# Summing gathered rows of v in runs of eight instead of four, beside the first half of the second block

## What is computed

```python
def peer_ffn(h, wq, sub_keys, u, v):
    def block(t):                                   # t: 128 tokens of width D = 1024
        ...                                         # 8 heads choose 16 experts each: idx, g
        a = jax.nn.gelu(jnp.einsum('tpkd,td->tpk', u[idx], t).astype(jnp.float32), approximate=False)
        return jnp.einsum('tpk,tpkd->td', (g * a).astype(t.dtype), v[idx])
```

## Time and profile before

| | us |
|---|---|
| median of 3 timed runs | 2850.53 |
| lowest and highest of them | 2850.36, 2853.51 |
| the profiled execution | 2857.94 |
| its span, first to last instruction | 2856.1 |
| TensorE busy with matmuls | 2311.2 (81%) |
| VectorE busy | 1887.5 (66%) |
| GpSimd busy | 1086.1 (38%) |
| all matmuls of L1939 (2048 records, tiles 0 to 3): idle time ahead of them for a landing | 271 |

### The profile page before, as it was taken

How to read it: one execution, slowest core, us unless ns; L and a number is a source line. 1 busy time by engine, 2 the same in 40 slices (tenths; PEclk the granted TensorE clock), 3 DMA queues, 4 the chain that set the end, 5 groups by cost and what they waited for, 6 DMA issues and landing times.

```text
span 2856.1 us, 43515 instructions
## 1 busy us (share of the span) xinstructions
PE 2311.2 (81%) x16384; PEld 1719.6 (60%) x16384; DVE 1887.5 (66%) x4182; ACT 899.6 (31%) x1615; POOL 1086.1 (38%) x1029
## 2 busy tenths in 40 slices
PE   7999988877565554665847988875999999999998
PEld 5787876445311010112736877622777999997998
DVE  3666885786565666537898877763444687667766
ACT  4555652111100000001013333322333455456544
POOL 0000002544466676667886676576555000000000
PEclk8999999988777787777968999867999999999999
DMA  7432126787799999999999999999999545662564
GB/s 303 152 124 85 38 83 246 288 335 282 298 374 374 356 376 355 336 356 342 401 359 400 404 408 409 410 376 337 388 391 408 194 155 191 189 210 89 184 189 152
DMA packets 225231, 810.32 MB, mean 284 GB/s; under 512 B 24704, under 2 KB 30720, under 8 KB 223232
## 3 DMA queue, kind: packets, MB, share of 16 engines
q0 software_dynamic: 147456, 536.94, 49.2%
q1 hardware_dynamic: 76992, 270.09, 26.5%
q10 hardware_dynamic: 576, 0.52, 0.1%
HBM read 805.35 MB, written 2.10 MB: 283 GB/s over the span
## 4 chain that ended last, share of the span: by engine, by line
PE 42%; DVE 17%; issue 11%; another core or an unknown queue 5%; DMA 5%; POOL 2%; ACT 1%; DVEq 0%; POOLq 0%; SPq 0%; ACTq 0%
PE ps L2004 10%; PE ps L2005 10%; PE ps L2006 9%; DVE pe_ring L2847 7%; PE ps L1939 6%; DMA pe_ring<-in_v,pe_vidx 2%; DMA pe_ring<-in_u,pe_idx 2%; PE ps L1894 1%; DVE la_w_lo L2900 1%; POOL pe_ring L1826 1%; PE ps L2087 1%; DVE pe_itop L2774 1%; POOL pe_ring L1832 1%; PE ps L2312 1%
## 5 line engine op out<-in xcount | busy, mean ns | idle before, releaser
L1826 POOL DMA_INDIRECT pe_ring<-in_u,pe_idx x415 | 462.6, 1115 | 297.4 <-issue 117.4
L1939 PE MATMUL ps<-pe_ring,pe_spot 128*32 128x512 f32 x1620 | 378.8, 728 | 172.3 <-DMA pe_ring<-in_v,pe_vidx 110.0
L1832 POOL DMA_INDIRECT pe_ring<-in_v,pe_vidx x405 | 417.1, 1030 | 224.0 <-issue 115.8
L2004 PE MATMUL ps<-la_h_hi,la_w_hi 128*128 128x256 f32 x1696 | 481.7, 284 | 9.6 <-issue 4.7
L2005 PE MATMUL ps<-la_h_lo,la_w_hi 128*128 128x256 f32 x1696 | 477.7, 282 | 2.9 <-issue 2.9
L2006 PE MATMUL ps<-la_h_hi,la_w_lo 128*128 128x256 f32 x1696 | 477.8, 282 | 2.6 <-issue 2.6
L2900 DVE TENSOR_TENSOR la_w_lo<-la_w_raw,la_w_hi 128x1024 fp32r<-128x1024 f32 (+1 forms) x348 | 415.5, 1195 | 87.6 <-ACT la_w_hi L2469 61.9
L2469 ACT ACTIVATE la_w_hi<-la_w_raw 128x1024 fp32r<-128x1024 f32 (+1 forms) x348 | 359.0, 1032 | 281.4 <-DMA la_w_raw<-in_down 89.0
L2004 PEld LDWEIGHTS ps<-la_h_hi,la_w_hi 128*128 128x128 f32 x1696 | 322.6, 190 | 38.0 <-issue 27.5
L2005 PEld LDWEIGHTS ps<-la_h_lo,la_w_hi 128*128 128x128 f32 x1696 | 320.2, 189 | 5.1 <-issue 4.8
L2006 PEld LDWEIGHTS ps<-la_h_hi,la_w_lo 128*128 128x128 f32 x1696 | 320.3, 189 | 3.9 <-issue 3.9
(11 more groups left out here) (409 smaller groups left out, 3911.5 us busy)
## 6 DMA issues: line engine op xcount, KB each, us to landing
la_w_raw<-in_gate SPq DMA_DIRECT2D x88, 512.0 KB
la_w_raw<-in_up SPq DMA_DIRECT2D x88, 512.0 KB
la_w_raw<-in_down SPq DMA_DIRECT2D x64, 448.0 KB
la_w_raw<-in_a_in SPq DMA_DIRECT2D x40, 512.0 KB
wring<-in_w_in SPq DMA_DIRECT2D x32, 512.0 KB
la_w_raw<-in_down SPq DMA_DIRECT2D x32, 512.0 KB
wring<-in_wq SPq DMA_DIRECT2D x22, 512.0 KB, 7.4
xT<-in_w_mod_rows SPq DMA_DIRECT2D x8, 1024.0 KB, 4.9
```

The source lines that it names most:

```text
L1826: pool.indirect_dma_start(row(n), None, io["u"], bass.IndirectOffsetOnAxis(idx[:, t, j:j + 1], 0)).then_inc(land[GATHERS[n][0]], 16)
L1832: pool.indirect_dma_start(row(n), None, io["v"], bass.IndirectOffsetOnAxis(vidx[:, t % 2, at:at + 1], 0)).then_inc(land[GATHERS[n][0]], 16)
L1939: return pe.matmul(ps[PER * grp:PER * grp + PER, half, :], spot[:, j // TOKENS % 2, grp, lo:lo + PER], row(n)[:, half * 512:(half + 1) * 5 ...
L2004: pe.matmul(slot(n), parts_hi[:, n % SPLIT, i, :], hi[:, k, :], start=first, stop=False)
```

## The change

`sums_beside` takes 16 runs of eight rows for each of the tiles 2 and 3 in place of 32 runs of four. A run is due when its eighth row is. The sums of tiles 0 and 1 stay as they are. `SQUARES_AT`, the row of tile 3 at which `add_squares(2)` is due, goes from 58 to 56, a multiple of eight.

```diff
--- before.py
+++ after.py
@@ -1446,7 +1446,7 @@
     CHOOSE_AT, CHOOSE_V = (25, 51, 77, 103), 9
     HEAD, IN_PSUM = 26, 8
     AHEAD, STEP, LAG = 14, 3, 5
-    TURN_AT, SUM_AT, SQUARES_AT = (96, 84), (16, 32), 58
+    TURN_AT, SUM_AT, SQUARES_AT = (96, 84), (16, 32), 56
 
     def gathers():
 
@@ -1971,9 +1971,9 @@
                 yield DOTTED[2] + 3 * STEP
                 turn_weights(2)
                 for t in (2, 3):
-                    for j in range(0, P, GROUPS):
-                        yield sum_at(t, j + GROUPS - 1)
-                        sum_rows(t, range(j, j + GROUPS))
+                    for j in range(0, P, 2 * GROUPS):
+                        yield sum_at(t, j + 2 * GROUPS - 1)
+                        sum_rows(t, range(j, j + 2 * GROUPS))
 
             def turns_beside():
                 yield DOTTED[3] + 3 * STEP
```

## The result

The changed kernel takes 2925.45 us (median of 6 runs, 2914.72 to 2928.76) against 2852.02 us of the kernel before (6 runs, 2842.53 to 2860.52). The ratio is 1.025 with a 95% interval of 1.0231 to 1.0269: 66 to 77 us slower, where 40 were forecast and 2925 was the upper end of the range. The profiled execution of the changed kernel took 2927.72 us (span 2925.9).

A forecast was written before the change was run, and what follows sets the result against it. Row transfers were taken to bound the kernel up to 1846 us, TensorE the last tile. Full stage +26, beside attention +19, last tile -5 made +40 on 2850.5: 2890 us, range 2843 to 2925.

The forecast's parts named there:

- 3 rows under way: In tile 2, when a run of eight's last row lands: 3 rows (3.8 us) may be under way, before 11 (14 us).

The follow-up runs named there:

- the later release: Against the changed kernel, a run of eight releases all its slots with its last matmul, not one by one; 1.03 times the kernel before.

## What to carry to other kernels

Where a ring of buffers feeds a stage that is full of transfers, count how many transfers may be under way at the moment a consumer gets its last one, and hold it against one turn: start to release, release to issue, issue to landing. Well above it fewer buffers cost nothing here (8 rows in place of 11), well below it each consumer run costs idle transfers (3.9 us each here), in every run of the full stage, also where no wait shows before the change. A consumer that is reached late takes from the same number, even if it finds all its rows landed. Joining two consumer steps takes from this number twice: the rows of the second step are no longer ahead, and those of the first are not given back.

## What the runs showed of the hardware

- A row lands with the last of the 16 DMA engines, and the others can be a row ahead. At 1749 us three rows were still to land, the last at 1752.7, and yet the DMA share was 0.35 from 1750 to 1751, 0.06 from 1751 to 1752, which is one engine of 16, and 0.01 from 1752 to 1753. So 3 rows under way kept the engines as a whole busy not for 3.8 us but for about 1.5. Why one engine came last is open.
- The Trainium skill ("DMA: Bandwidth & Descriptors", "Anatomy of one DMA") says that a semaphore is raised only once the write is confirmed, which takes most of 2 us. The trace does not bear out that length: the last packet of those rows ended at 1752.3, 0.4 us ahead of the last landing, and 0.4 to 0.5 us lay between the two at most other stops of the two traces of after and of the later release.
- The first row behind a stop took 3.8 to 5.8 us from issue to landing, where the data alone is 1.3 us at full rate. At 1754.87 and at about half of the other stops 1.6 us went by before its first packet moved; with the 0.4 us at the end that is about 2 us in which nothing moves, and the packets themselves took the rest.
- TensorE, which had stood for 11.5 us, began the run of 1749.03 at a granted clock of 0.50, the lower of its two levels (1.2 of 2.4 GHz), and was at 1.00 in the slice of 1754 to 1756: that run took 5.94 us in place of 3.64. So a run that has waited also gives its slots back later.
